# Six transposes of a layer in another place of the z stage of a fused two-block transformer kernel

## What is computed

```python
for l in range(DEPTH):                       # two layers
    h = _rms_norm(x, norm_g[l])
    proj = jnp.einsum('bsd,de->bse', h, w_in[l])
    q_a, k_a, v_a, z_a, c_q, c_kv, k_r, z_b = jnp.split(proj, split_points, axis=-1)
    ...
    o_a = _rms_norm(o_a, diff_subln_g[l]) * (1.0 - lambda_init)
    o_a = o_a.reshape(b, seq, DIFF_WIDTH) * jax.nn.silu(z_a)
    ...
    o_b = _mla_attention(q_nope, q_rope, k_nope, k_rope, v_b)
    o_b = o_b.reshape(b, seq, MLA_WIDTH) * jax.nn.silu(z_b)
    mixed = jnp.concatenate([o_a, o_b], axis=-1)
    x = x + jnp.einsum('bse,ed->bsd', mixed, w_out[l])
```

## Time and profile before

| | us |
|---|---|
| median of three runs | 1940.66 |
| profiled execution | 1940.85 |
| its span, first to last instruction | 1939.0 |
| PE busy | 1924.1 (99%) |
| DVE busy | 1426.3 (74%) |
| ACT busy | 1071.6 (55%) |

### The profile page before, as it was taken

How to read it: one execution, slowest core, us unless ns; L and a number is a source line. 1 busy time by engine, 2 the same in 40 slices (tenths; PEclk the granted TensorE clock), 3 DMA queues, 4 the chain that set the end, 5 groups by cost and what they waited for, 6 DMA issues and landing times.

```text
span 1939.0 us, 26713 instructions
## 1 busy us (share of the span) xinstructions
PE 1924.1 (99%) x9794; PEld 1631.0 (84%) x9794; DVE 1426.3 (74%) x2033; ACT 1071.6 (55%) x1569; POOL 46.3 (2%) x73
## 2 busy tenths in 40 slices
PE   8999999999999999999999999999999999999998
PEld 7888888888888888888888888888888888888886
DVE  7877675656777675656768766888877887888777
ACT  5545676654444676564544544555555555555554
POOL 1000030000000030000100000000000000000000
PEclk9999999999999999999999999999999999999999
DMA  8755455556665556545666455566666666676653
GB/s 310 235 201 171 142 156 158 143 163 183 201 206 177 144 154 181 154 152 183 211 194 187 153 168 189 181 188 184 194 186 193 186 189 188 190 244 199 222 184 122
DMA packets 246965, 357.09 MB, mean 184 GB/s; under 512 B 15318, under 2 KB 136496, under 8 KB 246364
## 3 DMA queue, kind: packets, MB, share of 16 engines
q1 hardware_dynamic: 245148, 349.08, 57.8%
q0 software_dynamic: 1584, 6.54, 1.0%
q10 hardware_dynamic: 144, 0.26, 0.0%
HBM read 352.69 MB, written 3.16 MB: 184 GB/s over the span
## 4 chain that ended last, share of the span: by engine, by line
PE 99%; DVE 1%; DMA 0%; ACT 0%; SPq 0%; issue 0%; ACTq 0%
PE acc L451 22%; PE acc L444 11%; PE acc L428 11%; PE acc L430 11%; PE acc L429 11%; PE acc L1174 4%; PE acc L1175 4%; PE acc L1176 4%; PE acc L1433 3%; PE acc L1435 3%; PE acc L1434 3%; PE aux L508 2%; PE aux L1105 1%; PE aux L1433 1%; PE aux L1435 1%; PE aux L1434 1%
## 5 line engine op out<-in xcount | busy, mean ns | idle before, releaser
L391 DVE TENSOR_TENSOR sb_w_lo<-sb_stage,sb_w_hi 128x1024 fp32r<-128x1024 f32 x477 | 584.3, 1228 | 272.5 <-ACT sb_w_hi L386 265.6
L386 ACT ACTIVATE sb_w_hi<-sb_stage 128x1024 fp32r<-128x1024 f32 x477 | 503.4, 1058 | 360.7 <-PE acc L444 122.9
L451 PE MATMUL acc<-sb_xT,sb_w_hi 128*128 128x512 f32 x1856 | 445.7, 391 | 0.0
L451 PEld LDWEIGHTS acc<-sb_xT,sb_w_hi 128*128 128x128 f32 x1856 | 340.8, 188 | 65.8
L444 PEld LDWEIGHTS acc<-sb_xT,sb_w_lo 128*128 128x128 f32 x1856 | 238.7, 191 | 9.3
L444 PE MATMUL acc<-sb_xT,sb_w_lo 128*128 128x256 f32 x1856 | 243.0, 283 | 0.0
L428 PE MATMUL acc<-sb_w_hi,sb_mT 128*128 128x512 f32 x560 | 224.7, 401 | 1.2 <-DVE sb_mT L531 1.2
L430 PE MATMUL acc<-sb_w_hi,sb_mT 128*128 128x512 f32 x560 | 218.6, 390 | 0.0
L429 PE MATMUL acc<-sb_w_lo,sb_mT 128*128 128x512 f32 x560 | 218.4, 390 | 0.0
L428 PE MATMUL acc<-sb_w_hi,sb_xT 128*128 128x512 f32 x384 | 155.9, 406 | 0.0
L430 PE MATMUL acc<-sb_w_hi,sb_xT 128*128 128x512 f32 x384 | 150.1, 391 | 0.0
(11 more groups left out here) (399 smaller groups left out, 2819.8 us busy)
## 6 DMA issues: line engine op xcount, KB each, us to landing
sb_stage<-w_in SPq DMA_DIRECT2D x232, 512.0 KB, 4.3
sb_stage<-w_up SPq DMA_DIRECT2D x176, 512.0 KB, 3.7
sb_stage<-w_out SPq DMA_DIRECT2D x96, 512.0 KB, 3.9
sb_stage<-w_down SPq DMA_DIRECT2D x60, 512.0 KB, 6.9
sb_pair_stage<-w_down SPq DMA_DIRECT2D x28, 512.0 KB, 6.4
sb_stage<-w_kv SPq DMA_DIRECT2D x16, 512.0 KB, 6.7
sb_kvb<-w_in SPq DMA_DIRECT2D x16, 512.0 KB, 5.9
sb_stage<-w_ukv SPq DMA_DIRECT2D x16, 512.0 KB, 3.8
```

The source lines that it names most:

```text
L386: act.activation(w_hi[:, j % RING, 0:size], stage[:, j % RING, 0:size], ACT.Copy).then_inc(hi_ready, 1)
L391: dve.tensor_tensor(w_lo[:, j % RING, 0:size], stage[:, j % RING, 0:size], w_hi[:, j % RING, 0:size].bitcast(F32), ALU.subtract).then_inc( ...
L451: mm = pe.matmul(acc[:, 2 * pair + c, :], hi[:, k, c * P:(c + 1) * P], both, start=first and k == 0, stop=last and k == 3)
```

## The change

Six of the eight gate turns of a layer are moved to other units, the numbers of the bank's uses are made to fit the new order, and the count that PE waits for before unit 0 of the out stage goes from 29 to 30. Group 0 moves from behind units 12 and 13 to 11 and 15, group 1 from 20 and 21 to 19 and 23, group 2 from 28 and 29 to 27 and 31. Group 3 stays behind units 4 and 5 of the out stage (36 and 37). No operation is added or taken away; the three engines read the same tables, so PE's transposes, ACT's rounding and DVE's rest all move.

```diff
-MLA_TB = [16, 17, 18, 21, 22, 25, 26, 29]
-GATE_TURN = {12: (0, 0, 19), 13: (0, 1, 20), 20: (1, 0, 23), 21: (1, 1, 24), 28: (2, 0, 27), 29: (2, 1, 28),
+MLA_TB = [16, 17, 18, 20, 22, 24, 26, 28]
+GATE_TURN = {11: (0, 0, 19), 15: (0, 1, 21), 19: (1, 0, 23), 23: (1, 1, 25), 27: (2, 0, 27), 31: (2, 1, 29),
              36: (3, 0, 30), 37: (3, 1, 31)}
...
                         if i == 0:
                             banks_free(pe, pairs, 20 + c)
                         if u in (0, 6):
-                            pe.wait_ge(tb_free, tb0 + (29 if u == 0 else 31))
+                            pe.wait_ge(tb_free, tb0 + (30 if u == 0 else 31))
                         product_rows(pe, base, U_QKV + 64 + u, mT, 2 * i, 2, 512, c % 2, i == 0, i == 7,
                                      (lambda: pe.wait_ge(tb_free, tb0 + 32)) if u == 6 else None)
```

## The result

The changed kernel takes 1949.43 us (median of six runs, 1947.73 to 1950.22), the kernel before 1940.66: a ratio of 1.0046, interval [1.0035, 1.0056], or 8.8 us more. The profiled execution of the changed kernel took 1949.22 us, with a span of 1947.4.

The account below looks back on a forecast made before the run. PE, busy 1924.1 of 1939.0 us, was taken to bound the kernel. 1940.85 + 6.60 for two waits - 0.54 saved on turns = 1946.91, with the median 0.19 lower, written as 1946.8 us; range 1945.3 to 1950.7.

Parts of the forecast that it names:

- What bounds the kernel: Whole run: PE is busy 1924.1 of 1939.0 us; DVE or ACT count only where they make PE wait.
- The turns on PE: z stage: a turn moved behind a head's scores saves PE 0.045 us, 0.54 us for 12 turns.
- The wait in front of the out stage: Before out unit 0: PE stands 3.30 us a layer for DVE's rest of the last turn, 6.60 us in all.
- The five other places: Other moved turns in the z stage: pushed ACT and DVE work makes PE wait nowhere; tightest reserve 0.64 us.
- A: Start of the out stage: the two waits of 3.30 us without a fall of the clock; 1946.8 us; chance 0.46.
- B: Start of the out stage: PE's clock falls, 1.9 us lost per fall; 1948.7 or 1950.6 us; chance 0.38.
- Hidden wait (D): Start of the out stage: DVE's rest is done in time, only the saving is left; 1940.1 us; chance 0.10.
- heads (C): Behind z units 18 and 26: late exponentials make PE stand 0.60 us, 2.4 us in all; 1949.2 us; chance 0.06.

Follow-up runs that it names:

- the divided wait: Changed kernel with PE's count before the out stage lowered to 26 and the count of 30 asked for before out unit 4; 1939.92 us.
- PE kept busy: Changed kernel with twelve more 128 x 512 products on PE behind the last turn, results thrown away; 1946.66 us.
- longer wait: Changed kernel with six 128 x 512 copies on DVE ahead of the rest of the last turn; 1956.80 us.
- second one: Changed kernel run once more, unaltered, for more executions; median 1949.83 us, its profiled execution 1950.25 us.
- the last turn alone: Kernel before with only turn (2,1) moved behind unit 31 and the count raised to 30; 1949.99 us.
- the other five: Changed kernel with the last turn (2,1) put back behind unit 29 and the count back at 29; 1940.57 us.

## Why the prediction was right, and where it wasn't

*What bounds the kernel.* Right: all of the loss is PE's, as waiting or as slower work, and the busy time of DVE, ACT and POOL didn't grow.

*The turns on PE.* Four units were to take 14.1 us everywhere; they take 14.11 and 14.12. The mean of before was (13.68 + 14.63) / 2 = 14.155, so a turn saves 0.035 to 0.045 us by the windows (forecast 0.045), 0.42 to 0.54 in all (forecast 0.54). The run with the divided wait has it alone: 0.46 us by the medians, within its interval of nothing.

*The wait in front of the out stage.* Right in place and order, and in size with a little luck. The product starts 413.86 - 410.18 - 0.36 = 3.32 us late in layer 0 and 861.83 - 858.15 - 0.36 = 3.32 in layer 1; forecast 3.30. The sum had 415.10 - 411.37 = 3.73 from the turn to the product, which are 3.68, and 0.43 for the turn itself, which is 0.36 here: two small misses that cancel. The chain was read from the earlier trace rows, none of which shows the wait: what the trace of before shows is the order on DVE, and the gap that the moved instruction drops into. That order, not the turn, is the price: with the rest two instructions earlier the wait is 1.31 us shorter, without the wait all of it is gone. It wasn't won back anywhere.

*The five other places.* Right: no wait there. At the tightest head the reserve was to be 0.64 us; it is 0.82, as in the earlier trace rows:

```profile
354.34 0.69 ACT L537 ACTIVATE sb_mT<-aux,sb_subln_l 128x512 fp32r<-128x512 f32 x1 [1.12 <-PE aux L508]
354.92 1.05 ACT L386 ACTIVATE sb_w_hi<-sb_stage 128x1024 fp32r<-128x1024 f32 x1
...
361.34 0.16 DVE L1979 RECIPROCAL sb_inv_sum<-sb_row_sum 128x2 f32<-128x2 f32 x1
...
362.32 0.49 PE L1086 MATMUL aux<-sb_ident,sb_s 128*128 128x128 f32 x3
```

ACT's next unit starts 0.58 us after the rounding does, not 0.69 as the sum had it; counted from the last scores, the exponentials start 0.46 us later than before, not 0.61, and PE's turn of the weights 0.44 later.

*The choice between A and B.* Here the forecast number failed: 1946.8 was for no fall of the clock, with 0.46, and in every execution of the changed kernel there is an excess over it; it is 2.8 us by the medians (1949.43 less 1946.66 with PE kept busy). B was the case, and I gave it 0.38. The step that failed is the sentence that the clock fell 3.0 us after PE's last work in the earlier trace rows and that my wait was about as long: from it I took a coin for each layer that mostly stays up. The traces have falls from 2.2 us (changed kernel, layer 0: from 410.78 to 413.0) to 4.1 us (longer wait, layer 1: from 860.87 to 865.0) after PE's last work, and some of them come when PE is already back; a wait can thus be over and still bring one. The size of a fall, 1.9 us from the earlier trace rows, was of the right order, and lies between those measured: 2.6 us for the fall during the wait, 2.4 each with the longer wait, 1.56 each for the two that came after the restart. With these the parts nearly close: 1939.92 with the divided wait, 6.64 for the two late starts and 2.6 for one fall make 1949.2, measured 1949.22 (first profile); with 3.1 for two late falls 1949.7, measured 1950.25 (second one), of which 0.6 stay open.

*Hidden wait (D), heads (C).* Neither, by the runs with the last turn alone and with the other five.

The Trainium skill (TensorE: Matmul & The Clock Gate, section "Why this matters for your kernels") warns that PE standing between bursts of matmuls goes back to the lower clock. The runs agree: with a wait of 1.77 us the profiled execution has no fall, and the times of the ten leave no room for one of 1.5 us or more; with 3.08 us each execution is at least 1.0 us over the kept-busy kernel, and each of the three profiled ones has a fall in a layer or in both; with 5.85 us the profiled one has a fall in both.

## What to carry to other kernels

When an instruction is moved to the last place before a stage that reads its result, read the order of the engine that writes that result: the wait is the work already queued in front of it there (here the maxima and two evacuations), whatever the moved step costs by itself. A count of a semaphore that stands for "everything up to here" should be asked for where the data are first read; dividing it made the move harmless. And price a wait of some 3 us on PE with the slower products behind it, not with its length alone.

## What the hardware showed beyond that

With the last turn alone, the clock fell after the wait had ended (at 414.3 and 861.4, against restarts at 414.14 and 861.05), so that a look at the clock during the wait alone would have found 1.00. Transposes of the identity, whose results nobody reads, kept it at 1.00 through the wait and behind it, and saved 3.0 us against the same kernel without them (1946.79 and 1949.83).
